# One attention stage of a two-block network: output weights prepared before the last exponentials, and the first head norm taken between two halves of the key operand

## What is computed

```
k, v = shared_kv(x, kv_norm, kv_w, k_norm)             # keys normalized per 64-wide half head
q = rms_norm((h @ w_q).reshape(b, t, 8, 2, 64), q_norm)
s = einsum("bqhcd,bkhcd->bhcqk", q, k) * scale + bias   # c: the two halves of a head
pm = softmax(where(causal, s, -1e30))
attn = pm[:, :, 0] - lam * pm[:, :, 1]
o = rms_norm(attn @ v, subln) * (1 - lam_init)
x = x + o.reshape(b, t, 1024) @ w_o
```

## Time and profile before

| | |
|---|---|
| median of 3 runs | 1317.06 us (1316.93 to 1318.77) |
| the profiled execution | 1317.06 us, of which the span from first to last instruction is 1315.3 us |
| PE busy | 1284.5 us (98%) |
| POOL busy | 1011.9 us (77%) |
| ACT busy | 686.0 us (52%) |
| DVE busy | 638.7 us (49%) |
| granted TensorE clock | 1.000 |

### The profile page before, as it was taken

One profiled execution on the slowest core, in us unless ns is written; L12 is line 12 of the kernel. 1 busy time (PEld: TensorE's weight loads), 2 busy tenths in 40 slices (PEclk: granted clock), 3 DMA queues, 4 the chain that ended last, 5 costly groups with the idle time before them and its releaser, 6 DMA issues.

```text
span 1315.3 us, 27704 instructions
## 1 busy us (share of the span) xinstructions
PE 1284.5 (98%) x10992; PEld 1233.1 (94%) x10992; DVE 638.7 (49%) x1151; ACT 686.0 (52%) x954; POOL 1011.9 (77%) x798
## 2 busy tenths in 40 slices
PE   8998999999999999999999999999999999999999
PEld 7888999999988889999998978999999999999998
DVE  8996655555546757555565574211113545311112
ACT  8834544444666665434456475444345666544342
POOL 5227988888776659898878894988887766988885
PEclk9999999999999999999999999999999999999999
DMA  6306665555544335555454442545554433555530
GB/s 271 130 33 226 192 235 175 191 187 173 183 154 140 132 120 189 178 189 187 170 186 158 170 156 93 192 172 185 191 178 150 160 129 129 192 173 180 191 128 32
DMA packets 33879, 217.07 MB, mean 165 GB/s; under 512 B 3683, under 2 KB 7428, under 8 KB 8196
## 3 DMA queue, kind: packets, MB, share of 16 engines
q1 hardware_dynamic: 30096, 211.14, 45.4%
q10 hardware_dynamic: 3700, 4.75, 1.5%
HBM read 213.26 MB, written 2.62 MB: 164 GB/s over the span
## 4 chain that ended last, share of the span: by engine, by line
PE 80%; DVE 11%; ACT 4%; issue 2%; POOL 1%; DMA 0%; DVEq 0%; ACTq 0%; POOLq 0%
PE up L1622 18%; PE up L1623 18%; PE up L1624 18%; PE acc L1622 7%; PE acc L1624 7%; PE acc L1623 7%; DVE opnd L1025 2%; ACT w_hi L533 1%; PE up L1757 1%; DVE s_work L1165 1%; DVE opnd L1180 1%; ACT opnd L694 1%; PE side L1630 1%; DVE s_work L1174 1%; PE acc L1992 0%
## 5 line engine op out<-in xcount | busy, mean ns | idle before, releaser
L424 POOL TENSOR_TENSOR w_lo<-ring,w_hi 128x512 fp32r<-128x512 f32 x740 | 945.0, 1310 | 222.9 <-ACT w_hi L533 219.9
L1622 PE MATMUL up<-opnd,w_hi 128*128 128x256 f32 x1984 | 569.4, 287 | 4.3 <-DVE opnd L1025 1.5
L1623 PE MATMUL up<-opnd,w_lo 128*128 128x256 f32 x1984 | 561.2, 283 | 0.0
L1624 PE MATMUL up<-opnd,w_hi 128*128 128x256 f32 x1984 | 561.2, 283 | 0.0
L533 ACT ACTIVATE w_hi<-ring 128x2048 fp32r<-128x2048 f32 x185 | 353.2, 1910 | 257.9 <-PE up L1624 202.3
L1622 PEld LDWEIGHTS up<-opnd,w_hi 128*128 128x128 f32 x1984 | 380.3, 192 | 16.8 <-issue 12.4
L1623 PEld LDWEIGHTS up<-opnd,w_lo 128*128 128x128 f32 x1984 | 380.4, 192 | 1.2 <-issue 1.0
L1624 PEld LDWEIGHTS up<-opnd,w_hi 128*128 128x128 f32 x1984 | 380.4, 192 | 0.0
L1622 PE MATMUL acc<-opnd,w_hi 128*128 128x256 f32 x816 | 232.1, 284 | 1.2 <-DVE x L1272 1.2
L1623 PE MATMUL acc<-opnd,w_lo 128*128 128x256 f32 x816 | 230.9, 283 | 0.0
L1624 PE MATMUL acc<-opnd,w_hi 128*128 128x256 f32 x816 | 230.9, 283 | 0.0
(11 more groups left out here) (307 smaller groups left out, 1453.5 us busy)
## 6 DMA issues: line engine op xcount, KB each, us to landing
ring<-in_stream SPq DMA_DIRECT2D x197, 1024.0 KB, 4.9
bias_rows<-mix ACTq DMA_DIRECT2D x1, 1536.0 KB
x<-in_x SPq DMA_DIRECT2D x1, 1024.0 KB, 5.7
mix<-in_s_b SPq DMA_DIRECT2D x1, 1024.0 KB, 7.7
mix<-in_s_c SPq DMA_DIRECT2D x1, 1024.0 KB, 11.7
mix<-bias_rows ACTq DMA_DIRECT2D x1, 1024.0 KB, 5.6
out_x<-x SPq DMA_DIRECT2D x8, 128.0 KB, 1.7
mix<-in_p ACTq DMA_DIRECT2D x2, 256.0 KB, 3.4
```

Of the source, the lines that this page charges most:

```text
L424: ins = nc.gpsimd.tensor_tensor(w_l[:, cols], ring[:, r, cols], w_h[:, cols].bitcast(f32), ALU.subtract)
L1622: MM(o, l_hi, r_hi, start=start, stop=False, skip_group_check=True)
L1623: MM(o, l_lo, r_hi, start=False, stop=False, skip_group_check=True)
L1624: return MM(o, l_hi, r_lo, start=False, stop=stop, skip_group_check=True)
```

## The change

Four things are changed. Output slot wo+2 gets a place of its own for its high part, over the head norms' temporaries; its low part stays in `w_lo[:, 1]`, so that POOL now waits itself until the last projection is done (`mm_done` at 62), and ACT waits until all eight head norms are applied (`qk_ready`). ACT makes the high parts of wo+2 and wo+3 both at t = 23, before the last head's exponentials, instead of at t = 24 and 25. At t = 2 ACT makes the high part of slot kvq+3 before the key operand, and of that operand only tiles 0 to 3; tiles 4 to 7 follow at t = 4, after the first root and the second square. DVE makes low tiles 4 to 7 at t = 4 instead of 3, after the second eviction and the first multiplication.

```diff
-        last_hi = {START["glu"] + 2: mix_r[:, 0:2048], START["glu"] + 3: mix_r[:, 10240:12288],
+        last_hi = {START["wo"] + 2: mix_r[:, 8192:10240],
+                   START["glu"] + 2: mix_r[:, 0:2048], START["glu"] + 3: mix_r[:, 10240:12288],
...
# POOL, low_part
+                if s == START["wo"] + 2:
+                    pool.wait_ge(sem("mm_done"), START["wo"])
                 if s == START["wo"] + 3:
                     pool.wait_ge(sem("diff_read"), 2 * HEADS)
...
# ACT, high_part
+                elif s == START["wo"] + 2:
+                    act.wait_ge(sem("qk_ready"), len(DIFF_NORMED))
                 elif s == START["wo"] + 3:
                     act.wait_ge(sem("diff_scores"), HEADS)
...
-            def new_operand(name, squares=True):
+            def new_operand(name, squares=True, tiles=range(KT)):
...
-                for m in range(KT):
+                for m in tiles:
...
# ACT, the stage's loop over t
             for t in range(2, DIFF_HALVES):
-                if t == 24:
-                    high_parts_to(S + 14)
...
                 for n in normed_at(t - 2):
                     diff_square(n)
                 if t == 2:
-                    new_operand("kv", squares=False)
+                    high_parts_to(S + 3)
+                    new_operand("kv", squares=False, tiles=range(4))
+                if t == 4:
+                    new_operand("kv", squares=False, tiles=range(4, KT))
                 if t % 2 == 0 and t < 24:
                     high_parts_to(S + t // 2 + 2)
-                if t == 25:
+                if t == 23:
                     high_parts_to(S + 15)
                 for h in heads_at(DIFF_AT, t - 1):
                     diff_exps()
...
# DVE, the stage's loop over t
-                if t in (2, 3):
-                    for m in range(4 * t - 8, 4 * t - 4):
+                if t in (2, 4):
+                    for m in range(2 * t - 4, 2 * t):
                         low_tile("kv", m)
```

## The result

The changed kernel took 1323.08 us (median of 6 runs, 1320.88 to 1324.55) beside 1317.12 for the kernel before (6 runs, 1316.93 to 1318.77): a ratio of 1.0039, 95% interval 1.0029 to 1.0049, slower by 5.1 us by that ratio and by 6.0 by the medians. The profiled execution is the longest of the six, 1324.55 us, with a span of 1322.6, which is 7.3 longer than the span before. This is where those 7.3 us lie, read in the order of time.

What follows compares the result with a forecast made beforehand. PE, busy 98% of the span, was taken to bound the kernel. Plus 2.3 (key operand), plus 2.6 (transposes), minus 1.5 (wo+3) made plus 3.4: 1320.5 us; range from 1316.1 taken down by 0.3 to 1322.5, own range 1318.9 to 1321.5.

Steps and rivals of the forecast that it cites:

- the pairing: Key operand's low tiles and last probabilities: each DVE instruction waits for the end of POOL's running subtraction, then they alternate.
- the clock rival: Matmuls after PE's 4.2 us idle before L2012 slow by 0.08 each: 2.0 added, 1322.5 us; chance 0.12.
- Part 1: Key operand: four low tiles meet POOL's released subtractions, so PE's second head-statistics matmul starts at 385.5, not 383.16: plus 2.3.
- Part 2, the transposes: Last head: probabilities meet busy POOL, so PE's transposes (L2012) start at 469.0 instead of 466.44: plus 2.6.
- the ceiling: Last probabilities, L1400 beside POOL: 1.33 each, as for L1025; taken for the sum.
- The floor: Last probabilities, L1400 beside POOL: only 0.35 to 0.48 each, transposes plus 0.7, whole sum plus 1.5.
- Part 2, wo+3: Output slot wo+3: POOL's low part is ready at about 470, before PE asks, so its wait goes: minus 1.5.
- no handover cost: Rival: DVE gets in beside POOL both times, all three PE waits go, 1312.5 us; chance 0.13.
- one place only: Rival: only the key operand's tiles or only the probabilities pay, 1316.1 or 1316.9 us; chance 0.19.
- A: At 383.16, PE's second head-statistics matmul waits 1.16 us for DVE's first normalized operand; worth 1.3.
- B: At 465.25, the values matmul of head 7 waits 1.61 us for ACT's copy L834; worth 1.8.
- C: At 475.50, output slot wo+3 waits 1.31 us for POOL's low part; worth 1.5.

Runs made afterwards that it cites:

- e2: Kernel before with only the high parts of wo+2 and wo+3 moved ahead of the last exponentials, key operand as before: 1320.49 us, ratio 1.0024.
- e1: Kernel before with only the key operand's edits (two halves behind the early high part of kvq+3), output slots as before: 1320.86 us, ratio 1.0021.
- e3: e1 with POOL waiting, before the low part of kvq+3, for the first four low tiles; later POOL slots written out: 1319.81 us, ratio 1.0011.
- e7: Kernel before with only the key operand split otherwise: six tiles, high part of kvq+3, root, second square, then two tiles: 1317.34 us, ratio 0.9995.
- e8: e2 with 28 throwaway transposes on PE ahead of the last head's transposes: 1319.34 us, ratio 1.0009.
- e4: e2 with POOL waiting, before the fourth subtraction of wo+2, for the last probabilities: 1314.70 us, ratio 0.9977.
- e6: e7 together with e4: 1315.57 us, ratio 0.9982.

## Why the prediction was right or wrong

The sign, the two places and the mechanism of the pairing held; the sum was too low. It gave 1320.5, plus 3.4. Measured were plus 5.1 by the ratio, which is 1322.2 and just inside the range (up to 1322.5), and plus 6.0 by the medians, 1323.08, which is 0.6 above it. The sum's own range, 1318.9 to 1321.5, leaves both out; what reaches that far is the clock rival, which set the top.

- **Part 1, plus 2.3: right.** Measured +2.2, with 1.37 a tile where 1.4 was taken. One detail was off: the cost shows as four short waits of PE for low tiles and not as one before the head statistics, because PE takes those tiles in step with DVE.
- **Part 2, the transposes, plus 2.6: nearly right.** Measured +2.2 to +2.3. All four instructions paid, as in the ceiling that was taken for L1400: 1.25 and 1.37 beside POOL. The floor (plus 0.7) is refuted.
- **Part 2, wo+3, minus 1.5: right.** Measured -1.7 in the traces of after and e2. The wait of L2026 for ACT's copy went too, as forecast, and brought nothing, since the transposes of the last head came later anyway.
- **The clock: the step that failed.** The prediction saw that PE would idle some 4.2 us, named the row at the start where matmuls after such a wait were slow, and gave this 0.12 on the ground that the granted clock was at nine tenths or more in every slice. That was no evidence: no wait of PE in this stage of before was longer than 1.61, so its page could not show what a longer one does. After a wait of 3.84 the clock fell in both traces that have it, and none of the 18 runs of after and e2 reached a mean of 1.000. The sum put this term at nothing; measured, it is 2.5 to 2.7. The rival's price, 2.0, was low by 0.5 to 0.7: the transposes run at the lower level as well, and in the trace of after the 24 matmuls lost 0.09 to 0.10 each instead of 0.08. The row that it was taken from was no sure ground either: the granted clock of before is 1.00 from 3 to 9 us, so what made those first transposes slow is not shown to be the clock.
- **The early fall of the clock,** 1.7 in the profiled execution, was not in the prediction at all. Runs of before lose clock too (14 of 33 at 0.999), though no trace shows where. Whether the edits make such losses more frequent stays open: beside the experiments 37 of 66 runs of before are at 1.000, and of the experiments without the long wait (e1, e3 to e7) 24 of 64.

With the clock added as measured, 1320.5 + 2.7 = 1323.2. That this meets the median is in part luck: the three terms measure +2.8, not +3.4, and some of the runs lost clock elsewhere too. Of the rivals, "no handover cost" and "one place only" fall with e1 and e2: each place pays alone. "The clock falls" happened, on top of the forecast as it was written.

The Trainium skill's "TensorE: Matmul & The Clock Gate", section "HAM oscillation — how this bites in real kernels", warns that an idle gap of PE in mid-kernel leaves the next matmuls at the lower clock. The traces of after and e2 agree, with 0.50 and 0.56 behind the wait, and that of e8, at 1.00 with the gap filled, does too.

## What to carry to other kernels

When an edit lets an engine start earlier, list what it will now run beside: here the edits were to remove waits worth 1.3 us (A) and 3.3 (B and C), and the pairing of POOL with DVE took back some 3.5 and 4. Hold the released engine by one wait until the short urgent instructions are through (e4), and look behind the hold for who pays instead (e3). Price every new idle stretch of PE with the matmuls that follow it at the lower clock, and don't read a clock that never had the occasion to fall as one that won't. Read it in several executions, if you can: behind one and the same wait it fell in some and not in others.

## What the runs showed of the hardware that was not expected

- **The clock falls after one single wait in mid-kernel.** Level 0.50 behind 3.84 us of idle PE, after some 80 us of nearly unbroken matmuls; waits of up to 1.61 in this stage left it at 1.00, and so did 28 throwaway transposes in place of most of the wait.
- **The clock also falls where nothing was edited.** In the profiled execution of after it was 0.93 and 0.90 in 40 to 60 us, in the first stage, which is the same code in both kernels. It fell behind a wait of PE of 1.58 to 2.14 us in five of the ten traces, and behind one of 1.27 to 1.86 at the same matmul it stayed full in the other five. Losses of clock divide the runs of before as well (1316.68 at 1.000, 1319.01 at 0.999), by almost as much as the 2.6 us that was taken to be measurable; where they lie in those runs no trace shows.
- **The pairing goes nearly one for one, and not for every instruction.** The four DVE instructions of the last probabilities, 0.35 to 0.48 with POOL idle, take 1.16 to 1.37 beside a run of POOL's subtractions (1.25 each), and a low tile of 0.41 takes 1.03 (e6) to 1.37. POOL's four stretch from 5.0 to between 5.05 and 5.53, so nearly all the loss is DVE's. L1390, with one input from the bank acc, took 0.68 with and without POOL.
